# Head pairs: GpSimd forms the low part of every weight tile in two operations of 512 columns in place of one of 1024

## The chip, the cores and the metric

The kernel runs on one core of one Trainium2 chip. The metric is the device time of one execution in microseconds (us). Before the change it is 1581.94 us, the median of three runs (1579.63 to 1582.36).

## The reference

Two blocks of a small model run one after the other on x of 512 tokens by 1024 features, all in float32. Only the first bears on the change:

```python
mod = silu(c) @ w_ada + b_ada                      # shift, scale, gate
h = rms_norm(x, norm_g) * (1.0 + scale) + shift
proj = h @ w_in
(hq, hf, hi, hz, rq, rk, rv, rz, ga, gb) = split(proj)
oA = hgrn2_chunkwise(silu(hq), hf, hi, lower_bounds)        # 8 heads, gated linear recurrence
uA = head_rms_norm(oA, hg_norm_g) * silu(hz)
oB = retention_chunkwise(rotary(rq), rotary(rk), rv)        # 8 heads, retention
uB = head_rms_norm(oB, ret_norm_g) * silu(rz)
m = sigmoid(ga) * uA + sigmoid(gb) * uB
x = x + gate * (m @ w_out)
```

The second block is a conformer convolution, a swiglu FFN, banded attention with sinks and another FFN; the change does not touch it.

## The kernel before

**Split products.** Every float32 weight is used as a sum of two rounded parts. A weight tile (a "chunk", 128 partitions by 1024 columns) is loaded by the sync queue into `w_raw[:, j]`, one of four slots j. ScalarE writes its rounded high part to `w_hi[:, j]` (L791). GpSimd writes the low part, `w_lo = w_raw - w_hi` (`w_low`, L665). TensorE then makes three products for each 128-column block of the chunk: high by high, high by low, low by high (`dense`, L2151 to L2153, features by tokens; `dense_tokens`, L2209 to L2211, which takes two chunks at once and waits for both).

**The stream.** Chunk c sits in slot c mod 4. The semaphore `lo_ready[j]`, which GpSimd raises when a low part is written, does two things: it lets TensorE start on the chunk, and it lets the sync queue load the next chunk into the slot. ScalarE writes a high part when the load has landed (`raw_in[j]`) and TensorE has let go of the slot (`tile_done[j]`). Each engine's order is written out by hand.

**Head pairs.** The first block runs over four pairs of heads, p = 0 to 3, as a loop on each engine. A pair has 20 chunks. Chunks 8 and 9 are taken by VectorE alone, so GpSimd forms the low parts of the others in the order of `LOW_ORDER`: 3, 4, 5, 6, 7, 12, 10, 11, 13 to 19, and then the first three of what comes next (20, 21, 22). That is 18 tiles in a pair and 72 in the loop. Between them stand four 512-column operations (`head_low`, L675) for the head norms: behind chunk 16, behind chunk 17 and two behind chunk 20.

**The place in the middle of a pair.** TensorE's order there is chunk 6, 7, 12, then `hgrn_levels(0)` (L2312), then `dense_tokens` of chunks 10 and 11. The level products are cut over four banks. The first bank waits for the first two levels that VectorE's second loop makes, and the second bank for that loop's last level:

```python
if n < 2:
    pe.wait_ge(prep_done, p * 6 + (3 * e + n + 1))
```

VectorE meanwhile runs `decayed(0)`: seven products of `packed` and `q` (L1509), seven of `packed` and `key` (L1514), the last of which raises `prep_done`, then `k_far` (L1517), a copy of two columns (L1519), `q_far` (L1520), and after it the rotary products L1629, L1630 and L1631. Nearly all of these read two tensors in SBUF. L1631 waits for VectorE's own L1630 to finish; none of the others in this run waits for VectorE itself. ScalarE writes the high part of chunk 10, copies, and then that of chunk 11.

**After the pairs.** GpSimd makes `lead_hi` and `lead_lo` (L684 and L686) behind chunk 22 of the last pair, for the first block of `w_out` on TensorE (L2162).

Of the kernel before, what the change touches and what calls it, by code (L numbers as in the profile page):

```python
# [16 lines left out]
F32 = mybir.dt.float32  # L17
# [3 lines left out]
ALU = mybir.AluOpType  # L21
# [3 lines left out]
T = 512  # L25
# [3 lines left out]
SLOTS = 4  # L29
# [93 lines left out]
PAIR_CHUNKS = 20  # L123
# [5 lines left out]
def phase_starts():  # L129

    sizes = [("pairs", PAIRS * PAIR_CHUNKS), ("w_out", KC), ("pw1", 2 * KC), ("pw2", KC)]
    for layer in range(2):
        if layer == 1:
            sizes += [("kv", 4), ("q", KC), ("w_o", KC)]
        sizes += [(f"up{layer}", 2 * FF_PAIRS), (f"down{layer}", KC)]
    at, starts = 0, {}
    for name, n in sizes:
        assert n % SLOTS == 0
        starts[name] = at
        at += n // SLOTS  # L140
    return starts, at

START, QUADS = phase_starts()
# [47 lines left out]
def program(nc, weights, ada_in, xT, x_turned, vec_in, sinks_in, rel_in, ret_tab, lvl_in, eye_in, tri_in, hot_in, ident_in, taps_in,  # L192
            rel_scratch, glu_scratch, outT):
    ctx = ExitStack()
    with ctx:
        def sb(name, shape, dt=F32, where=ctx):
            return where.enter_context(nc.sbuf_tensor(name, shape, dt))

        def sem(name):
            return ctx.enter_context(nc.semaphore(name))  # L200
# [4 lines left out]
        w_raw = sb("w_raw", [P, SLOTS, D])  # L205
        w_hi = sb("w_hi", [P, SLOTS, D], F32R)
        w_lo = sb("w_lo", [P, SLOTS, D], F32R)
# [129 lines left out]
        hi_ready = [sem(f"hi_ready{j}") for j in range(SLOTS)]  # L337
        lo_ready = [sem(f"lo_ready{j}") for j in range(SLOTS)]
# [318 lines left out]
        def _(pool):  # L657
            TT = nc.gpsimd.tensor_tensor
# [3 lines left out]
            def w_low(I, j):  # L662

                pool.wait_ge(hi_ready[j], I + 1)
                TT(w_lo[:, j, :], w_raw[:, j, :], w_hi[:, j, :].bitcast(F32), ALU.subtract).then_inc(lo_ready[j], 1)  # L665
# [5 lines left out]
            with pool.Fori(0, PAIRS) as p:  # L671
                def head_low(e, r):

                    pool.wait_ge(osq_high, p * 4 + (2 * e + r + 1))
                    TT(osq_lo[:, r, :], hbuf[:, 2 + r, :], osq_hi[:, r, :].bitcast(F32), ALU.subtract).then_inc(osq_low, 1)  # L675

                for c in LOW_ORDER:
                    w_low(p * (PAIR_CHUNKS // SLOTS) + (START["pairs"] + c // SLOTS), c % SLOTS)
                    for e, r in HEAD_LOW_AFTER.get(c, ()):
                        head_low(e, r)  # L680

# [686 lines left out]
        def _(dve):  # L1368
# [401 lines left out]
            def taps(plan):  # L1770

                for c, k, b, last in plan:
# [7 lines left out]
                    else:  # L1780
# [3 lines left out]
                        else:  # L1784
                            STT(conv[:, c, :], src, w, bank, ALU.mult, ALU.add).then_inc(conv_done, 1)

            bank_of = {c: b for run in TAP_PLAN for c, _, b, _ in run}

            def halves_in(c):
# [342 lines left out]
        def _(pe):  # L2132
# [491 lines left out]
            def ffn(layer_n, norm, x_mix, hidden):  # L2624
# [14 lines left out]
                for part in range(MIXED_PARTS):  # L2639
                    lead_down, last_down = (FF_ORDER.index(("down", part, m)) for m in (0, KC // 2 - 1))  # L2640
                    quads(at, lead_down // 2)
                    for n in range(lead_down // 2 * 2, last_down // 2 * 2 + 2):
                        if n == lead_down:
                            pe.wait_ge(hid_low, mixed_at(layer_n, part + 1, 0))
                        kind, _, _ = FF_ORDER[n]
                        seven_products(f0 + n, up + n // 2, n % 2, own_x if kind == "down" else x,
                                       mixes=mixes_before(layer_n, part) if n == lead_down else None)
                    at = last_down // 2 + 1
# [292 lines left out]
```

## Time and profile before

| what | value |
|---|---|
| median of three runs | 1581.94 us (1579.63 to 1582.36) |
| the profiled execution's own time | 1578.51 us |
| its span, first to last instruction | 1576.7 us |
| TensorE busy | 1544.0 us, 98% |
| GpSimd busy | 884.3 us, 56% |
| VectorE busy | 1134.5 us, 72% |
| mean granted TensorE clock | 0.995 of full speed |
| the four head pairs | about 59 to 541 us |

A row of a timeline gives the start in us from the span's start, the duration in us, the engine, the line of the program, the operation, what it writes and reads, the shapes, and in brackets the idle time of the engine before it with what ended that time. "x7" are seven instructions of one line merged into one row. An instruction's duration runs from its start to its end and holds any time in which it was held up inside the engine.

### The profile page before, as it was taken

To read this page: it belongs to the slowest core of one execution; us is meant where nothing else is said; L and a number is where in the kernel's file an instruction comes from. 1 tells how busy PE (TensorE), PEld (TensorE's weight loads), DVE (VectorE), ACT (ScalarE), POOL (GpSimd) and SP (SyncE) were. 2 spreads that over 40 slices of the span, in tenths; PEclk is the share of its full clock that TensorE was granted. 3 is DMA by queue.
4 is the path that set the end of the run, shared out by engine and by line. 5 is a ranking of instruction groups with operands and counts; after the bars stand their busy time and mean duration, and the time that the engine had idled before them with its cause. 6 is when DMAs were issued, how large, how long until landed. Compare 5 with 4: busy or idle time off the path is not lost.

```text
span 1576.7 us, 28481 instructions
## 1 busy us (share of the span) xinstructions
PE 1544.0 (98%) x10803; PEld 1372.8 (87%) x10803; DVE 1134.5 (72%) x1782; ACT 881.7 (56%) x1480; POOL 884.3 (56%) x523
## 2 busy tenths in 40 slices
PE   6999999999999999999999999999999999999997
PEld 4888888888888878568999999988788899999996
DVE  7887587597687869977766766754666766776755
ACT  4555455355355545477664665554667666566553
POOL 1444344445435448827777777654115678677653
PEclk8999999999999999999999999999999999999999
DMA  9422322322323455712333333353112333333332
GB/s 375 144 94 81 121 81 94 120 79 94 116 76 99 136 98 166 188 41 94 107 107 108 107 104 101 104 177 103 54 42 68 98 103 107 106 97 105 108 119 68
DMA packets 53659, 173.12 MB, mean 110 GB/s; under 512 B 5403, under 2 KB 11580, under 8 KB 53052
## 3 DMA queue, kind: packets, MB, share of 16 engines
q1 hardware_dynamic: 47296, 159.90, 32.0%
q10 hardware_dynamic: 6268, 11.95, 3.2%
q8 instruction: 59, 0.97, 0.3%
q14 instruction: 36, 0.29, 0.1%
HBM read 165.48 MB, written 6.36 MB: 109 GB/s over the span
## 4 chain that ended last, share of the span: by engine, by line
PE 79%; DVE 3%; issue 2%; ACT 2%; POOL 2%; DVEq 0%; ACTq 0%; POOLq 0%
PE gps L2151 9%; PE gps L2153 9%; PE gps L2152 9%; PE gps L2588 8%; PE gps L2590 8%; PE gps L2589 8%; PE aps L2588 4%; PE aps L2589 4%; PE aps L2590 4%; PE gps L2511 2%; PE gps L2209 2%; PE gps L2210 1%; PE gps L2211 1%; POOL w_lo L665 1%; PE aps L2678 1%
## 5 line engine op out<-in xcount | busy, mean ns | idle before, releaser
L665 POOL TENSOR_TENSOR w_lo<-w_raw,w_hi 128x1024 fp32r<-128x1024 f32 x140 | 361.1, 2584 | 472.5 <-ACT w_hi L791 472.4
L2151 PE MATMUL gps<-xa_hi,w_hi 128*128 128x512 f32 x639 | 256.8, 402 | 2.5 <-DVE xa_lo L1453 2.5
L2153 PE MATMUL gps<-xa_hi,w_lo 128*128 128x512 f32 x639 | 250.2, 392 | 0.0
L2152 PE MATMUL gps<-xa_lo,w_hi 128*128 128x512 f32 x639 | 250.2, 392 | 0.0
L791 ACT CAST w_hi<-w_raw 128x1024 fp32r<-128x1024 f32 x140 | 146.3, 1045 | 98.6 <-DMA w_raw<-weights_dram 41.7
L2151 PEld LDWEIGHTS gps<-xa_hi,w_hi 128*128 128x128 f32 x639 | 120.5, 189 | 30.5 <-DVE xa_lo L1453 4.1
L2153 PEld LDWEIGHTS gps<-xa_hi,w_lo 128*128 128x128 f32 x639 | 120.6, 189 | 26.2
L2152 PEld LDWEIGHTS gps<-xa_lo,w_hi 128*128 128x128 f32 x639 | 120.8, 189 | 22.6
L1855 DVE TENSOR_TENSOR sums<-aps,sums 128x512 fp32r<-128x512 f32 x58 | 40.1, 692 | 138.4 <-ACT sums L1111 138.4
L746 POOL TENSOR_TENSOR w_lo<-diff,w_hi 128x512 fp32r<-128x512 f32 x60 | 77.7, 1295 | 110.0 <-ACT w_hi L1117 110.0
L740 POOL TENSOR_TENSOR w_lo<-w_raw,w_hi 128x512 fp32r<-128x512 f32 x60 | 92.7, 1545 | 41.6 <-ACT w_hi L1094 41.5
L2151 PE MATMUL gps<-xb_hi,w_hi 128*128 128x512 f32 x250 | 98.4, 394 | 0.0
L2153 PE MATMUL gps<-xb_hi,w_lo 128*128 128x512 f32 x250 | 97.4, 390 | 0.0
L2152 PE MATMUL gps<-xb_lo,w_hi 128*128 128x512 f32 x250 | 97.3, 389 | 0.0
L1845 DVE TENSOR_TENSOR sums<-aps,sums 128x1024 fp32r<-128x1024 f32 x58 | 70.8, 1221 | 17.1 <-ACT sums L1106 16.8
L744 POOL TENSOR_TENSOR w_lo<-w_raw,w_hi 128x512 fp32r<-128x512 f32 x60 | 78.5, 1309 | 0.0
L743 POOL TENSOR_TENSOR diff<-w_raw 128x512 f32<-128x512 f32 x60 | 78.5, 1308 | 0.0
L748 POOL TENSOR_TENSOR w_lo<-w_raw,w_hi 128x512 fp32r<-128x512 f32 x60 | 78.1, 1301 | 0.0
L2588 PE MATMUL gps<-x_blocks,w_hi 128*128 128x256 f32 x264 | 75.5, 286 | 0.0
L2590 PE MATMUL gps<-x_blocks,w_lo 128*128 128x256 f32 x264 | 74.7, 283 | 0.0
L2589 PE MATMUL gps<-x_blocks,w_hi 128*128 128x256 f32 x264 | 74.7, 283 | 0.0
L2209 PE MATMUL gps<-w_hi,xa_hi 128*128 128x256 f32 x256 | 72.8, 284 | 1.8 <-POOL w_lo L665 1.7
(495 smaller groups left out, 5120.9 us busy)
## 6 DMA issues: line engine op xcount, KB each, us to landing
w_raw<-weights_dram SPq DMA_DIRECT2D x268, 512.0 KB, 3.6
ada_w<-ada_in_dram SPq DMA_DIRECT2D x8, 1024.0 KB, 18.6
gates<-ret_tab_dram ACTq DMA_DIRECT2D x4, 1024.0 KB, 6.9
spread<-glu_scratch_dram SPq DMA_DIRECT2D x12, 270.0 KB, 5.0
rel_scratch_dram<-rel_rows ACTq DMA_DIRECT2D x1, 3072.0 KB, 34.5
x<-x_turned_dram SPq DMA_DIRECT2D x2, 1024.0 KB, 7.4
res<-xT_dram ACTq DMA_DIRECT2D x1, 2048.0 KB, 10.3
bias<-rel_scratch_dram ACTq DMA_DIRECT2D x1, 2048.0 KB, 9.1
```

What stands on the lines that cost most here:

```text
L665: TT(w_lo[:, j, :], w_raw[:, j, :], w_hi[:, j, :].bitcast(F32), ALU.subtract).then_inc(lo_ready[j], 1)
L740: TT(lo["w11"], raw["w11"], hi["w11"].bitcast(F32), ALU.subtract).then_inc(first_low, 1)
L743: TT(diff[:], raw["w11"], raw["diff"], ALU.subtract).then_inc(diff_made, 1)
L744: TT(lo["w12"], raw["w12"], hi["w12"].bitcast(F32), ALU.subtract).then_inc(lo_ready[2 * s], 1)
L791: nc.scalar.copy(w_hi[:, j, :], w_raw[:, j, :]).then_inc(hi_ready[j], 1)
L2151: mm(gps[:, j, :], w_hi[:, j, w], x[0][:, k, :], start=k == 0, stop=False)
L2152: mm(gps[:, j, :], w_hi[:, j, w], x[1][:, k, :], start=False, stop=False)
L2153: last = mm(gps[:, j, :], w_lo[:, j, w], x[0][:, k, :], start=False, stop=k == blocks - 1)
L2209: mm(out, x[0][:, k, tok], wh, start=k == 0, stop=False)
L2588: mm(out, highs[s][name][:, w], x[name](k, 0), start=start and k == 0, stop=not start, **more)
L2589: mm(out, highs[s][name][:, w], x[name](k, 1), start=False, stop=not start, **more)
L2590: last = mm(out, lows[s][name][:, w], x[name](k, 0), start=False, stop=not start or k == HALF - 1, **more)
```

## The change

In the loop over the head pairs each low part is written by two operations on the two halves of the columns (T is 512). The wait ahead of the first and the semaphore behind the last stay. The tiles outside the loop, and the four `head_low` operations, are as they were.

```diff
+                def w_low_by_halves(I, j):
+
+                    pool.wait_ge(hi_ready[j], I + 1)
+                    TT(w_lo[:, j, 0:T], w_raw[:, j, 0:T], w_hi[:, j, 0:T].bitcast(F32), ALU.subtract)
+                    TT(w_lo[:, j, T:], w_raw[:, j, T:], w_hi[:, j, T:].bitcast(F32), ALU.subtract).then_inc(lo_ready[j], 1)
+
                 for c in LOW_ORDER:
-                    w_low(p * (PAIR_CHUNKS // SLOTS) + (START["pairs"] + c // SLOTS), c % SLOTS)
+                    w_low_by_halves(p * (PAIR_CHUNKS // SLOTS) + (START["pairs"] + c // SLOTS), c % SLOTS)
```

## Rows read from the trace of the kernel before

**Rows 1.** The page: busy time by engine, and the low parts' group.

```profile
PE 1544.0 (98%) x10803; PEld 1372.8 (87%) x10803; DVE 1134.5 (72%) x1782; ACT 881.7 (56%) x1480; POOL 884.3 (56%) x523
...
L665 POOL TENSOR_TENSOR w_lo<-w_raw,w_hi 128x1024 fp32r<-128x1024 f32 x140 | 361.1, 2584 | 472.5 <-ACT w_hi L791 472.4
```

**Rows 2.** Busy time by engine in the stretch of pair 1.

```profile
179.00:300.00 121.00, 119.21 (x788) 102.48 (x788) 90.81 (x135) 60.02 (x76) 56.44 (x23) 1.00 0.31 97
```

**Rows 3.** Waits of TensorE in the pairs: in total, times, longest (us).

```profile
PE gps L2209 <- POOL w_lo L665: 1.7, 1, 1.7
PE gps L2162 <- POOL osq_lo L686: 0.9, 1, 0.9
```

**Rows 4.** Timeline of GpSimd: low parts with little beside them, pair 0's end.

```profile
142.51 2.54 POOL L675 TENSOR_TENSOR osq_lo<-hbuf,osq_hi 128x512 fp32r<-128x512 f32 x2 [2.83 <-ACT osq_hi L883]
145.01 2.41 POOL L665 TENSOR_TENSOR w_lo<-w_raw,w_hi 128x1024 fp32r<-128x1024 f32 x1
```

**Rows 5.** Timeline of GpSimd: chunk 11 of pair 0, chunks 10 and 11 of pair 2.

```profile
80.87 3.88 POOL L665 TENSOR_TENSOR w_lo<-w_raw,w_hi 128x1024 fp32r<-128x1024 f32 x1 [1.60 <-ACT w_hi L791]
...
316.92 2.51 POOL L665 TENSOR_TENSOR w_lo<-w_raw,w_hi 128x1024 fp32r<-128x1024 f32 x1 [2.85 <-ACT w_hi L791]
321.03 3.91 POOL L665 TENSOR_TENSOR w_lo<-w_raw,w_hi 128x1024 fp32r<-128x1024 f32 x1 [1.59 <-ACT w_hi L791]
```

**Rows 6.** Timeline of VectorE in the same place of pair 2.

```profile
315.08 4.72 DVE L1509 TENSOR_TENSOR packed<-packed,q 128x256 f32<-128x256 f32 x7 [0.99 <-ACT hbuf L875]
319.72 2.50 DVE L1514 TENSOR_TENSOR packed<-packed,key 128x256 f32<-128x256 f32 x7
...
322.61 2.35 DVE L1519 COPY tile_decay<-hbuf 128x2 f32<-128x2 f32 x1
```

**Rows 7.** Timeline of GpSimd: chunks 10 and 11 of pair 1.

```profile
196.13 5.83 POOL L665 TENSOR_TENSOR w_lo<-w_raw,w_hi 128x1024 fp32r<-128x1024 f32 x1 [2.85 <-ACT w_hi L791]
...
201.91 3.95 POOL L665 TENSOR_TENSOR w_lo<-w_raw,w_hi 128x1024 fp32r<-128x1024 f32 x1
```

**Rows 8.** Timeline of VectorE in the same place of pair 1.

```profile
194.28 2.51 DVE L1509 TENSOR_TENSOR packed<-packed,q 128x256 f32<-128x256 f32 x7 [0.99 <-ACT hbuf L875]
...
199.60 2.38 DVE L1519 COPY tile_decay<-hbuf 128x2 f32<-128x2 f32 x1
201.90 0.55 DVE L1520 TENSOR_TENSOR q_far<-q,hbuf 128x384 f32<-128x384 f32 x1
...
202.97 0.68 DVE L1630 TENSOR_TENSOR rqk<-rqk,gates 128x512 f32<-128x512 f32 x1
203.68 2.72 DVE L1631 TENSOR_TENSOR rqk<-rqk,unit 128x512 f32<-128x512 f32 x1
```

**Rows 9.** Timeline of TensorE around the tokens of chunks 10 and 11, pairs 0 to 2.

```profile
82.15 3.29 PE L2312 MATMUL aps<-packed 128*128 128x128 f32 x28
85.20 0.36 PE L2209 MATMUL gps<-w_hi,xa_hi 128*128 128x256 f32 x1
...
206.11 0.36 PE L2209 MATMUL gps<-w_hi,xa_hi 128*128 128x256 f32 x1 [1.67 <-POOL w_lo L665]
...
323.40 1.85 PE L2312 MATMUL aps<-packed 128*64 128x64 f32 x56
325.19 0.38 PE L2209 MATMUL gps<-w_hi,xa_hi 128*128 128x256 f32 x1
```

**Rows 10.** Timeline of ScalarE: the high part of chunk 11 in pair 2.

```profile
319.90 1.05 ACT L791 CAST w_hi<-w_raw 128x1024 fp32r<-128x1024 f32 x1
```

**Rows 11.** Timeline of GpSimd in pair 0: an operation that follows another without a pause.

```profile
114.86 1.46 POOL L675 TENSOR_TENSOR osq_lo<-hbuf,osq_hi 128x512 fp32r<-128x512 f32 x1
```

**Rows 12.** Timeline of VectorE in pair 0 beside it, and its two-column copy undisturbed.

```profile
112.58 2.61 DVE L1509 TENSOR_TENSOR packed<-packed,q 128x256 f32<-128x256 f32 x1
...
115.11 1.58 DVE L1509 TENSOR_TENSOR packed<-packed,q 128x256 f32<-128x256 f32 x1
...
125.03 0.15 DVE L1519 COPY tile_decay<-hbuf 128x2 f32<-128x2 f32 x1
```

**Rows 13.** Timeline of GpSimd behind the last pair: `lead_lo`.

```profile
511.06 1.81 POOL L686 TENSOR_TENSOR osq_lo<-mixed,osq_hi 128x512 fp32r<-128x512 f32 x1
```

## The prediction

> **What bounds the kernel now.** I read the busy times of the page first [rows 1]: TensorE works 98% of the span, so time is lost or won only where TensorE waits. GpSimd is busy for 56%, and its low parts (140 tiles, 72 of them in the pairs, the rest outside) idle 472 us in front of themselves, nearly all of it waiting for ScalarE's high part. Read alone, this says that GpSimd has room and that a slightly dearer low part costs nothing. In the stretch of pair 1 TensorE is busy 119.2 of 121 us and GpSimd 56.4 [rows 2]. The waits of TensorE in all four pairs are two of any size: 1.7 us for a low part, once, and 0.9 us behind the last pair for `lead_lo` [rows 3].
>
> The one wait leads to the place that matters: the tokens of chunks 10 and 11. In pair 1 the low part of chunk 11 ends at 201.91 + 3.95 = 205.86 and TensorE goes on at 206.11, 0.25 to 0.26 later, after 1.67 us idle [rows 7, 9]. In pair 2 it ends at 321.03 + 3.91 = 324.94 and TensorE goes on at 325.19 [rows 5, 9]: the same 0.25, though no idle time shows. So this low part arrives just in time there, with no slack; pair 3 repeats pair 2. In pair 0 it ends at 84.75 and TensorE goes on at 85.20, a slack of about 0.2 [rows 5, 9]. Every delay here is paid in full, four times. All other low parts in the pairs end 3 us or more before their use; the two 512-column operations behind chunks 16 and 17 have over 1 us.
>
> **Why chunk 11 is late.** ScalarE has its high part at 319.90 + 1.05 = 320.95 in pair 2 [rows 10]. An unhindered low part takes 2.41 [rows 4], yet this one takes 3.91. VectorE tells why: its copy of two columns takes 2.35 us there, against 0.15 in another place [rows 6, 12], and both end together at 324.96. The two engines shut each other out while both read SBUF. GpSimd got its turn only when VectorE reached the copy at 322.61; the copy then waited out GpSimd. VectorE's instructions before it follow each other without a pause (14 of 0.41 us at a spacing of 0.34, plus `k_far`); I call this a train. A GpSimd operation that meets a train has two fates. In pair 2 chunk 10 comes at 316.92 and is let in at once (2.51), and the seven L1509 take 4.72 in place of 2.51 [rows 5, 6, 8]. In pair 1 it comes at the same offset from the train's start (1.85) and is kept out for the whole train, until the copy at 199.60: 5.83 [rows 7, 8]. Chunk 11, right behind it, loses again: `q_far`, L1629 and L1630 pass, and it gets in at 203.65, where L1631 waits for its predecessor and leaves a gap (L1631 then takes 2.72). These two fates set the price of a second operation.
>
> **The change, part by part.** *Work added.* Two operations of 512 columns back to back take 2.54 with nothing beside them, one of 1024 takes 2.41 [rows 4]: 0.13 more, 72 times, 9 us of GpSimd's time. Away from chunks 10 and 11 it is hidden behind TensorE's products, by the slacks above.
>
> *The second half must win its turn again.* Two outcomes stand in the trace. (a) One VectorE instruction slips in: at 114.86 a GpSimd operation follows another, the L1509 that was blocked finishes at 112.58 + 2.61 = 115.19, the next (115.11) is blocked for 1.58, and GpSimd's operation takes 1.46 in place of 1.27 [rows 4, 11, 12]. The tile then costs 1.3 + 1.46 = 2.75, about 0.3 more. (b) The train passes: chunk 11 of pair 1, above, lost 203.65 - 201.95 = 1.7 us [rows 7, 8].
>
> *Chunk 10 in pairs 0, 2 and 3.* The blocked instruction is a 256-column product, as in (a), so I take (a): it ends 0.3 later, which nobody waits for, since ScalarE's high part holds back chunk 11 until 320.95. VectorE's total block stays near 2.3, as it does one instruction in between.
>
> *Chunk 11 in pairs 0, 2 and 3.* If it still comes in at the copy, the first half ends 1.25 after 322.61, at 323.86. Behind the copy is the very situation of pair 1, so (b): `q_far`, L1629, L1630, 1.7 us; the second half runs from 325.56 to 326.8, 1.85 later than now. With (a) it is one `q_far` (0.5) and 0.1: 0.55 later. If chunk 11 is instead let in inside the train (the train stands 0.1 us elsewhere than before, which can turn the outcome), it is early, but the last L1514 is blocked about 2.4 us, from 322.2 to 324.6. The second bank of levels needs it after 16 of 56 products, at 323.40 + 0.47 = 323.87 [rows 9]: 0.7 us late. In pair 0 TensorE needs it at 82.15 + 8 of 28 products (0.9) = 83.05 and would get it at 84.4: 1.4 us. So the cost is 0.55 at the least and 1.85 at the most, by either way; I take 1.1, between the ends, three times: 3.3 us.
>
> *Pair 1.* If chunk 10 is kept out again until 199.60, its halves and those of chunk 11 need four turns instead of two. With (a) each time it ends about 0.3 later than now. With (b) each time: first half to 200.85, second from 202.55 (behind L1630) to 203.8, chunk 11 from the next gap at 205.5 to 206.8, and from the gap behind that (207.4) to 208.7: 2.8 later than 205.86. I take 1.3.
>
> *The rest of the pair.* Chunk 7's low part blocks VectorE's scans and chunk 12's a one-column addition; halves hold the port as long in all, and I put this at 0, at most 0.1. The loads behind `lo_ready` are 0.1 to 0.3 us later, hidden since ScalarE's high parts wait for TensorE to free the slot. Behind the last pair `lead_lo` takes 1.81 because it waits for a VectorE product [rows 13]; a start 0.25 later ends at the same time. Bounds: 0 and 0.3; I take 0.
>
> *Sum.* 3.3 + 1.3 = 4.6 us. The profiled execution's own time is 1578.51 (span 1576.7, and 1.8 around it); it becomes 1583.1. The median of the runs lies 3.4 above that execution, so the forecast is 1581.9 + 4.6 = 1586.5.
>
> **A rule beside it.** The Trainium skill, "SBUF — State Buffer", section "SBUF: two separate sides", says of the ports that VectorE and GpSimd share: whoever starts first has them for the whole instruction, and the other is fully blocked. By that rule, the lock free at each instruction's end, a half would wait for one VectorE instruction and never for a train. The copy's 2.35 us agree with the rule, chunk 10 of pair 1 does not: ten VectorE instructions passed it.
>
> **The rivals.** *One instruction only.* If each half waits for a single VectorE instruction, outcome (a) holds everywhere: 0.4 us in pair 0, 0.55 in pairs 2 and 3, 0.3 in pair 1, together 1.8: 1583.7, not to be told from no change. For it: the row at 114.86, which its repetitions in the later pairs confirm. Against it: both low parts of pair 1. This is also what the rule above would give.
>
> *The other side: not slower.* The change shifts when GpSimd asks, and whether chunk 10 is let in at once in pair 1 hangs on a few hundredths of a us. If it is, and the halves of chunk 11 fit in without delay, pair 1's 1.67 us go and nothing comes: 1580.3. It decides once chunk 11 ends no later than 0.25 us before TensorE's need in all pairs. All idle time of TensorE that GpSimd causes in the pairs is 1.7 + 0.9 = 2.6 us, so more than 0.2% (3.2 us) is out of reach.
>
> *The train wins always.* The second half of chunk 10 loses to the train too, in pairs 0, 2 and 3: it gets in at the copy (about 321.5) and ends at 322.75; then chunk 11's first half waits for the gap behind L1630 (324.5) and its second for the next one (327.6), ending at 328.9. That is 3.9 us a pair, with pair 1's 2.8 together 14.5: 1596.4. For it: the 5.83 us row. Against it: 114.86.
>
> **How the numbers follow.** 0.2% (3.2 us) is about what a measurement of this kernel can tell from no change. The forecast, a loss of 1.5 to 8 us, has 0.55, of which a fifth lies under 3.2. The rivals near no change (-1.7 to +1.5, with 1583.7 at their edge) have 0.25 together. The train has 0.15. I leave 0.05 for faster by more than 3.2, which no row supports. Slower is 0.44 + 0.15 = 0.59, same 0.11 + 0.25 = 0.36. The forecast's own range is 1583.4 to 1590; with the cases on both sides the range is 1580.5 to 1594.
>
> **What the profile would show.** Right: L665 in two forms, 144 instructions of about 1.3 us in the pairs; new waits of `dense_tokens` for `w_lo` in pairs 0, 2 and 3, of 0.5 to 1.9 us, or waits of L2312 for L1514 in their place; second halves of 2.5 to 3 us where they lose. Wrong: second halves of 1.3 to 1.5 us throughout and no new wait (the first rival); the L1509 group of 4.72 back at 2.5 to 3.6 with a second half of over 3 us (the last). What would make the prediction wrong is above all the arbitration, which four places of one execution show, and whose outcome turned with nothing visible between pairs 1 and 2.

## The result and the profile after

The changed kernel takes 1582.69 us in the median of 18 runs, the kernel before, run beside it on the same chip, 1579.24 in the median of 18 (1576.49 to 1582.36). The ratio is 1.0019, with a 95% interval of 1.001 to 1.0028: 3.0 us slower, between 1.6 and 4.4. That is a loss, but a small one, just inside the 0.2% that I had called no difference. Two of the 18 executions, of 1687.83 us (mean granted clock 0.849) and 3066.96 us, are left out of the ratio (the median of the other 16 is 1582.08), and nothing found below explains them.

The profiled execution after took 1586.11 (span 1584.3), the one before 1578.51 (span 1576.7). These two differ by 7.6 us, more than the medians do. Much of what follows is about why. First the page of the kernel after, the lines that answer to [rows 1], and its table of costliest groups:

```profile
PE 1544.6 (97%) x10803; PEld 1374.8 (87%) x10803; DVE 1111.6 (70%) x1782; ACT 881.7 (56%) x1480; POOL 907.7 (57%) x595
...
L665 POOL TENSOR_TENSOR w_lo<-w_raw,w_hi 128x1024 fp32r<-128x1024 f32 x68 | 166.6, 2456 | 222.3 <-ACT w_hi L797 222.2
L680 POOL TENSOR_TENSOR w_lo<-w_raw,w_hi 128x512 fp32r<-128x512 f32 x72 | 111.5, 1549 | 239.3 <-ACT w_hi L797 238.9
L681 POOL TENSOR_TENSOR w_lo<-w_raw,w_hi 128x512 fp32r<-128x512 f32 x72 | 109.8, 1525 | 0.0
```

The change was made: 144 halves, of 1.54 us on average where two back to back with nothing beside them take 1.27 [rows 4]. GpSimd is busy 23.4 us longer and VectorE 22.9 us shorter: a blocked VectorE instruction counts as busy, and short halves block it for less. All lines behind the change stand 6 lower (L1509 is now L1515, L1514 is L1520, L1519 is L1525, L2209 is L2215, L2312 is L2318).

Waits of TensorE in the pairs, after, as in [rows 3] (total, times, longest, in us), for the stretch from 54 us on, which begins a little earlier than mine of before did:

```profile
PE gps L2215 <- POOL w_lo L681: 6.9, 3, 2.8
PE gps L2168 <- POOL osq_lo L692: 1.0, 1, 1.0
PE aps L2318 <- DVE packed L1520: 0.4, 1, 0.4
```

Three waits for the second half of a low part where before had one. The timeline of TensorE places them: pair 0's first tokens, then chunks 10/11 of pair 1 (which waits for VectorE instead) and of pair 2. Pair 3, at 450.46 with 2.77, repeats pair 2.

```profile
55.38 0.35 PE L2215 MATMUL gps<-w_hi,xa_hi 128*128 128x256 f32 x1 [1.30 <-POOL w_lo L681]
...
204.57 1.39 PE L2318 MATMUL aps<-packed 128*64 128x64 f32 x40 [0.36 <-DVE packed L1520]
205.89 0.39 PE L2215 MATMUL gps<-w_hi,xa_hi 128*128 128x256 f32 x1
...
327.48 0.36 PE L2215 MATMUL gps<-w_hi,xa_hi 128*128 128x256 f32 x1 [2.78 <-POOL w_lo L681]
```

**Chunks 10 and 11, pair 1: let in.** GpSimd's timeline, then VectorE's, to be held against [rows 7] and [rows 8]:

```profile
197.02 1.42 POOL L680 TENSOR_TENSOR w_lo<-w_raw,w_hi 128x512 fp32r<-128x512 f32 x1 [2.71 <-ACT w_hi L797]
198.40 1.55 POOL L681 TENSOR_TENSOR w_lo<-w_raw,w_hi 128x512 fp32r<-128x512 f32 x1
201.12 1.30 POOL L680 TENSOR_TENSOR w_lo<-w_raw,w_hi 128x512 fp32r<-128x512 f32 x1 [1.17 <-ACT w_hi L797]
202.38 1.47 POOL L681 TENSOR_TENSOR w_lo<-w_raw,w_hi 128x512 fp32r<-128x512 f32 x1
```

```profile
198.72 5.80 DVE L1520 TENSOR_TENSOR packed<-packed,key 128x256 f32<-128x256 f32 x7
204.44 0.55 DVE L1523 TENSOR_TENSOR k_far<-key,hbuf 128x384 f32<-128x384 f32 x1
204.91 0.16 DVE L1525 COPY tile_decay<-hbuf 128x2 f32<-128x2 f32 x1
```

Chunk 10 gets in at once, and chunk 11 gets in too, inside VectorE's train. It is early, done at 203.85. The two halves stretch the seven L1520 to 5.80 us; TensorE's second bank of levels waits 0.36 for the last of them. The 1.67 of before are gone here.

**Pair 2: kept out.** GpSimd's timeline against [rows 5], VectorE's against [rows 6]:

```profile
316.31 4.74 POOL L680 TENSOR_TENSOR w_lo<-w_raw,w_hi 128x512 fp32r<-128x512 f32 x1 [2.71 <-ACT w_hi L797]
321.01 2.87 POOL L681 TENSOR_TENSOR w_lo<-w_raw,w_hi 128x512 fp32r<-128x512 f32 x1
323.84 1.71 POOL L680 TENSOR_TENSOR w_lo<-w_raw,w_hi 128x512 fp32r<-128x512 f32 x1
325.51 1.71 POOL L681 TENSOR_TENSOR w_lo<-w_raw,w_hi 128x512 fp32r<-128x512 f32 x1
```

```profile
316.90 2.51 DVE L1520 TENSOR_TENSOR packed<-packed,key 128x256 f32<-128x256 f32 x7
...
319.80 1.28 DVE L1525 COPY tile_decay<-hbuf 128x2 f32<-128x2 f32 x1
320.99 0.55 DVE L1526 TENSOR_TENSOR q_far<-q,hbuf 128x384 f32<-128x384 f32 x1
```

The first half of chunk 10 waits for the whole train, until the copy at 319.80. Then the second half loses again: three VectorE instructions pass and it takes 2.87. This is outcome (b) of the prediction, but on chunk 10. The halves of chunk 11 let one 512-column instruction by each (1.71), and end at 327.22; TensorE goes on 0.26 later.

The starts of TensorE's tokens serve as marks for a whole run. T4 is the first matmul of the tokens of chunks 4/5 of a pair, T10 that of chunks 10/11. The distances (differences of starts in TensorE's timeline, us) split the whole 7.6:

```
                 T4 of 0 |pair 0|10->4 |pair 1|10->4 |pair 2|10->4 |pair 3|10->lead|rest
before             54.22 |30.98 |89.44 |31.48 |89.34 |29.74 |89.36 |29.75 |68.63   |1063.8
after              55.38 |30.99 |89.21 |30.31 |89.00 |32.59 |90.41 |32.58 |69.80   |1064.1
after - before     +1.16 | 0.0  |-0.23 |-1.17 |-0.34 |+2.85 |+1.05 |+2.83 |+1.17   |+0.2
```

The kept-out pairs 2 and 3 cost 2.85 and 2.83 themselves, and the stretches behind them 1.05 and 1.17 more, where the same stretches behind pairs 0 and 1 are shorter than before. The experiments take these columns one by one.

### The profile page after: what moved, and what is told of

Same layout as the page of the kernel before. It is cut to its first block, busy times and chain, and to the rows that moved or that the text cites. A ratio compares the mean times of both kernels' runs of the same rounds, so it can differ in the third digit from the quotient of the medians.

```text
span 1584.3 us, 28553 instructions
## 1 busy us (share of the span) xinstructions
PE 1544.6 (97%) x10803; PEld 1374.8 (87%) x10803; DVE 1111.6 (70%) x1782; ACT 881.7 (56%) x1480; POOL 907.7 (57%) x595
## 4 chain that ended last, share of the span: by engine, by line
PE 65%; DVE 3%; ACT 2%; issue 1%; POOL 1%; DMA 0%; ACTq 0%; DVEq 0%
PE gps L2594 8%; PE gps L2596 8%; PE gps L2595 8%; PE gps L2157 6%; PE gps L2159 6%; PE gps L2158 6%; PE aps L2594 4%; PE aps L2595 4%; PE aps L2596 4%; PE gps L2517 2%; PE aps L2684 1%; PE aps L2694 1%; PE gps L2706 1%; PE gps L2215 1%; PE gps L2217 1%
## 5 line engine op out<-in xcount | busy, mean ns | idle before, releaser
L665 POOL TENSOR_TENSOR w_lo<-w_raw,w_hi 128x1024 fp32r<-128x1024 f32 x68 | 166.6, 2456 | 222.3 <-ACT w_hi L797 222.2
L680 POOL TENSOR_TENSOR w_lo<-w_raw,w_hi 128x512 fp32r<-128x512 f32 x72 | 111.5, 1549 | 239.3 <-ACT w_hi L797 238.9
L746 POOL TENSOR_TENSOR w_lo<-w_raw,w_hi 128x512 fp32r<-128x512 f32 x60 | 92.7, 1545 | 41.5 <-ACT w_hi L1100 41.5
L681 POOL TENSOR_TENSOR w_lo<-w_raw,w_hi 128x512 fp32r<-128x512 f32 x72 | 109.8, 1525 | 0.0
L2215 PE MATMUL gps<-w_hi,xa_hi 128*128 128x256 f32 x256 | 74.2, 290 | 6.9 <-POOL w_lo L681 6.9
L750 POOL TENSOR_TENSOR w_lo<-w_raw,w_hi 128x512 fp32r<-128x512 f32 x60 | 78.5, 1309 | 0.0
L754 POOL TENSOR_TENSOR w_lo<-w_raw,w_hi 128x512 fp32r<-128x512 f32 x60 | 78.1, 1302 | 0.0
L2594 PE MATMUL gps<-x_blocks,w_hi 128*128 128x256 f32 x264 | 75.5, 286 | 0.0
```

The costliest lines, as they stand in the source:

```text
L680: TT(w_lo[:, j, 0:T], w_raw[:, j, 0:T], w_hi[:, j, 0:T].bitcast(F32), ALU.subtract)
L681: TT(w_lo[:, j, T:], w_raw[:, j, T:], w_hi[:, j, T:].bitcast(F32), ALU.subtract).then_inc(lo_ready[j], 1)
L746: TT(lo["w11"], raw["w11"], hi["w11"].bitcast(F32), ALU.subtract).then_inc(first_low, 1)
L2215: mm(out, x[0][:, k, tok], wh, start=k == 0, stop=False)
L2594: mm(out, highs[s][name][:, w], x[name](k, 0), start=start and k == 0, stop=not start, **more)
```

## Experiments

Each group of kernels was run beside the kernel before, whose medians were 1577.81 (e1 to e4, 25 runs), 1579.85 (e5 to e8, 35) and 1579.11 (e9 to e11, 17); each ratio is against the runs beside it, with its 95% interval in brackets.

**1 and 2. Halves at chunks 10 and 11 alone, and everywhere but there.** The edits in GpSimd's loop over `LOW_ORDER`:

```
-                    w_low_by_halves(p * ..., c % SLOTS)
+                    low = w_low_by_halves if c in (10, 11) else w_low      # e1
+                    low = w_low_by_halves if c not in (10, 11) else w_low  # e2
+                    low(p * ..., c % SLOTS)
```

> Only chunks 10 and 11 are written in two halves (8 of the 72 tiles); the others in one operation as before. My theory after the two traces: the loss of the change has two parts, one at chunks 10 and 11 (a pair whose chunk 10 is kept out by VectorE's train costs 2.8 us of TensorE's time where it cost 1.7, a pair whose chunk 10 is let in costs 0 to 0.4 where it cost 0) and one at chunks 4 and 5 of pair 0 (1.2 us). This kernel has the first part alone: about 2 us above the kernel before in the median, a spread of single executions of about 8 us and more (it was 6 before), no wait of 1.3 us at the first tokens of pair 0. Rival, the cost is in the number of operations (each adds 0.13 us or more somewhere): 8 of 72 tiles give 0.3 us.

> All tiles but chunks 10 and 11 in halves (64 of 72). My theory: the 1.2 us at chunks 4 and 5 of pair 0 remains, the kept-out pairs cost 1.7 us each as before: 1.2 us above the kernel before, the spread of single executions about 6 us as before, a wait of 1.2 to 1.3 us at the first tokens of pair 0. Rival, the cost is in the number of operations: 2.7 us, nearly all of the change's loss.

Measured: halves at 10 and 11 alone 1584.05 us (6 runs), ratio 1.0042 [1.0029, 1.0055]; everywhere else 1578.5 (12 runs), 1.0002 [0.9994, 1.0011]. So the loss sits in eight of the 72 tiles. That there are more operations costs nothing as a whole: the 64 other tiles, split, leave the time where it was. In e1 pair 0 was kept out (its waits, from the timeline of TensorE):

```profile
89.86 0.35 PE L2216 MATMUL gps<-w_hi,xa_hi 128*128 128x256 f32 x1 [2.43 <-POOL w_lo L681]
```

That pair 0 takes 33.66 from T4 to T10, 2.68 more than before. In e10 below, where the other tiles are in halves too, a kept-out pair 0 takes only 31.51, with a wait of 0.28: VectorE's train starts 18.49 us behind T4 there and 20.67 in e1, so most of the same delay falls before TensorE's need.

The other three pairs of e1 were let in: 30.32 to 30.33 from T4 to T10, 0.58 above the 29.74 of a whole-tile pair that is let in. I had expected e1 about 2 us above the kernel before; the ratio says 6.6 (4.6 to 8.7). It lacks the gain described next, and its kept-out pair 0 is dear; measured terms and a chance give 5.1 for it (see the sum near the end).

Two things in e2 I had not expected. Pair 0's first tokens wait 1.30 there as in the kernel after, and in e1 they don't (0.13). And the stretches from T10 to the next T4 take 88.94 to 89.18, 0.3 to 0.4 less than before. The one hides the other in e2's ratio.

**3 and 4. A pause in the train.** VectorE waits for its own seventh product before the eighth, in the kernel before (e3) and after (e4):

```
-PAIR_STEPS = 29
+PAIR_STEPS = 31
...
-                        TT(q_part, q_part, right(qe, level), ALU.mult)
+                        last = TT(q_part, q_part, right(qe, level), ALU.mult)
+                    own.done(last)
```

> The kernel before, with one wait more on VectorE: behind the seventh product L1509 VectorE waits for its end before L1514 starts, in both uses of the function. My theory, that an operation of GpSimd which misses its turn is kept out until VectorE pauses: the train of 15 instructions now has a pause behind the seventh, so chunk 10 gets in at the latest 0.5 us after it asks, no low part of chunk 10 takes more than 3.2 us (5.8 was seen), TensorE's wait of 1.7 us is gone from every pair, and the times lie near the lowest of the kernel before: 2 to 3 us below its median, with a spread of single executions of 2 us or less in place of 6. Rival, the spread and the wait come from something else (loads, ScalarE): the median and the spread stay, or the pause itself costs TensorE 0.1 to 0.5 us a pair.

> The changed kernel with the same pause on VectorE. My theory: no pair is kept out, so what is left of the change is the 1.2 us at pair 0's first tokens and 0 to 0.4 us a pair where the last L1514 comes late for the second bank of levels: 1 to 2.5 us above the kernel before with the pause, about 0.5 us below the kernel before, spread 2 us or less. Rival, the kept-out pairs are no cause: 3 us above the kernel before, with the spread of the changed kernel (11 us).

Measured: e3 1582.81 (7 runs), 1.0029 [1.0018, 1.004], slower and not faster; e4 1579.61 (11 runs), 1.0012 [1.0003, 1.0021]. I had expected both below the kernel before, e3 by 2 to 3 us and e4 by 0.5; both lie above it, e4 by 1.9 (0.5 to 3.3). In both, all four pairs were let in at once. In e4 that took the spread of the runs from 10.8 us (1578.36 to 1589.11, the two left out aside) to 2.3 (1578.73 to 1581.04): the spread of the kernel after is mostly the fate of chunk 10. In e3 another thing came up. Timelines of GpSimd and VectorE, pair 2:

```profile
319.28 2.52 POOL L665 TENSOR_TENSOR w_lo<-w_raw,w_hi 128x1024 fp32r<-128x1024 f32 x1 [2.85 <-ACT w_hi L791]
323.39 2.50 POOL L665 TENSOR_TENSOR w_lo<-w_raw,w_hi 128x1024 fp32r<-128x1024 f32 x1 [1.59 <-ACT w_hi L791]
```

```profile
317.44 4.73 DVE L1509 TENSOR_TENSOR packed<-packed,q 128x256 f32<-128x256 f32 x7 [0.99 <-ACT hbuf L875]
322.20 4.70 DVE L1515 TENSOR_TENSOR packed<-packed,key 128x256 f32<-128x256 f32 x7
```

Now the whole chunk 11 also gets in inside the train, and the product that it blocks is the one that TensorE needs: waits of 1.18 in pair 0 and 0.51 in the others. The prediction had priced this case at 1.4 and 0.7. An early low part is no gain where the one who pays for it is later.

**5, 6 and 7. Both turns given by hand.** On top of the pause, GpSimd waits for VectorE's last product of the first head before chunk 11, so it starts at the copy as in [rows 5, 6]. e5 has whole tiles, e7 halves for all but 3, 4 and 5, e6 halves for all but 3, 4, 5, 10 and 11:

```
+                    if c == 11:
+                        pool.wait_ge(prep_done, p * 6 + 2)
+                    low = w_low_by_halves if c not in (3, 4, 5, 10, 11) else w_low  # e6
+                    low = w_low_by_halves if c not in (3, 4, 5) else w_low          # e7
```

> The kernel before (no halves) with two waits more: VectorE pauses behind the seventh L1509, and GpSimd starts the low part of chunk 11 only when VectorE's last L1514 of the first head is done. My theory: the fates of both low parts are fixed now. Chunk 10 is let in at once in all four pairs (as with the pause alone), chunk 11 gets in at the copy of two columns behind the train, so the last L1514 is not late (the 0.7 us a pair and 1.4 in pair 0 of the pause alone are gone) and chunk 11 ends as in the let-in pairs of the kernel before. From the first tokens of a pair to its second tokens: 31.0 us in pair 0 and 29.7 to 29.8 in the others, none at 31.5. Time: 1.67 us below the profiled execution of the kernel before at the same start-up, about 1577 us, or 1579 where TensorE's first sums run at the lower granted clock (1.9 us, a matter of chance in every kernel). Rival, the order is not what costs: as the kernel with the pause alone, 1582.8 us.

> The same two waits, and the halves for all chunks but 3, 4, 5, 10 and 11. My theory: the halves cost where two of them must win their turn against VectorE on the path to TensorE (chunks 4 and 5 of pair 0, chunks 10 and 11), and gain about 0.35 us a pair elsewhere (from the second tokens of a pair to the first of the next: 89.0 in place of 89.35 us), so this version keeps the gain alone: 1 to 1.5 us below the kernel before with the two waits, 2 to 3 us below the kernel before, spread of single executions about 2 us. Rival, the 0.35 us come with something else of the two halved kernels: no gain over the two waits alone.

> As the last one, but chunks 10 and 11 in halves too; the only difference is how many turns these two need. This puts my prediction's step to the test: the first half of chunk 11 gets in at the copy, behind which q_far, L1629 and L1630 follow without a pause. If a train passes a waiting GpSimd (outcome b of the prediction), the second half comes 1.7 us later and TensorE waits 1.7 to 1.9 us in each pair, 6 to 8 us in all, more if TensorE's clock falls behind the waits. If one instruction passes (outcome a), 0.5 us a pair, 2 us in all. The second half behind the copy in the kept-out pairs of the changed kernel took 2.87 us, so I expect the first.

Measured (12 runs each): e5 1579.36, 0.9993 [0.9983, 1.0003]; e6 1576.64, 0.9985 [0.9975, 0.9995]; e7 1582.85, 1.0019 [1.0009, 1.0029]. The step from e6 to e7 is the disputed one by itself: halves for chunks 10 and 11, with both turns fixed. Timelines of GpSimd and VectorE in e7, pair 2:

```profile
323.38 1.54 POOL L680 TENSOR_TENSOR w_lo<-w_raw,w_hi 128x512 fp32r<-128x512 f32 x1 [2.45 <-DVE packed L1524]
324.88 2.85 POOL L681 TENSOR_TENSOR w_lo<-w_raw,w_hi 128x512 fp32r<-128x512 f32 x1
```

```profile
323.69 1.26 DVE L1529 COPY tile_decay<-hbuf 128x2 f32<-128x2 f32 x1
324.87 0.54 DVE L1530 TENSOR_TENSOR q_far<-q,hbuf 128x384 f32<-128x384 f32 x1
325.33 0.68 DVE L1639 TENSOR_TENSOR unit<-unit,gates 128x512 f32<-128x512 f32 x1
325.94 0.68 DVE L1640 TENSOR_TENSOR rqk<-rqk,gates 128x512 f32<-128x512 f32 x1
326.65 1.64 DVE L1641 TENSOR_TENSOR rqk<-rqk,unit 128x512 f32<-128x512 f32 x1
```

The second half, right behind the first, loses to three instructions and takes 2.85; TensorE waits 1.63, the same in pairs 1 and 3. From T4 to T10 it is 31.43 against 29.83 in e6: 1.6 us a pair. The medians differ by 6.2 us, of which the four pairs give 5.2. Outcome (b) stands, at its price, where chunk 11 comes in at the copy. In pair 0 the wait is 0.14 only, and the stretch 31.37 against 30.99.

e6 beats both kernels, by 0.15% the one before (interval 0.05% to 0.25%). Its only wait for GpSimd in the pairs is the 0.9 for `lead_lo`. Against e5 it shows what halves are worth where they do no harm. The place is VectorE's `gates` product at L1665 (L1672 in e6). Timelines of GpSimd and VectorE in e5, pair 2:

```profile
367.63 2.37 POOL L665 TENSOR_TENSOR w_lo<-w_raw,w_hi 128x1024 fp32r<-128x1024 f32 x1 [3.82 <-ACT w_hi L793]
```

```profile
368.50 2.05 DVE L1665 TENSOR_TENSOR gates<-gates,unit 128x512 f32<-128x512 f32 x1
...
376.87 0.74 DVE L1563 COPY_PREDICATED at_near<-eye_mask,aps 128x512 f32<-128x512 int32 x1 [0.26 <-DVE at_near L1550]
```

and in e6:

```profile
364.95 1.29 POOL L680 TENSOR_TENSOR w_lo<-w_raw,w_hi 128x512 fp32r<-128x512 f32 x1 [3.74 <-ACT w_hi L800]
366.19 1.73 POOL L681 TENSOR_TENSOR w_lo<-w_raw,w_hi 128x512 fp32r<-128x512 f32 x1
```

```profile
365.91 0.88 DVE L1672 TENSOR_TENSOR gates<-gates,unit 128x512 f32<-128x512 f32 x1
...
373.15 0.74 DVE L1570 COPY_PREDICATED at_near<-eye_mask,aps 128x512 f32<-128x512 int32 x1 [0.26 <-PE aps L2322]
```

A whole tile blocks the product for 2.05 us, a half for 0.88. Between the product's start and the end of the `eye` copy lie 9.11 us in e5 and 7.98 in e6, and in e6 the copy no longer waits for VectorE itself but for TensorE. The attention behind it starts earlier: from T10 to the next T4 88.94 in e6, 89.31 to 89.32 in e5 (pairs 1 and 2), and behind the last pair 68.29 against 68.62. TensorE shows the same place: behind T10 of pair 2 its matmuls keep step in the two kernels, until `aps<-at_r,val` some 52 us later, which starts 0.3 us earlier in e6, and from the next one on 0.36. The medians of e5 and e6 differ by 2.7 us, twice the 1.3 that the four stretches give: the runs of each kernel fall in two groups about 2 us apart (a matter of the start, see below), and 7 of 12 runs of e5 but 5 of 12 of e6 are in the upper one.

**8. The kernel after with chunks 3, 4 and 5 whole.** The edit is `c not in (3, 4, 5)` alone, with no pause and no wait.

> The changed kernel with chunks 3, 4 and 5 in one operation again (60 of 72 tiles in halves), nothing else. My theory: the wait of 1.3 us at the first tokens of pair 0 falls to 0.1, the rest stays as in the changed kernel: 1.2 us below it in the median, a wide spread as there (10 us), since each pair whose chunk 10 is kept out still costs 2.8 us, and 1.4 more for a lower granted clock behind the wait. Rival: the wait at the first tokens of pair 0 has another origin and stays.

Measured: 1580.05 (12 runs, 1577.08 to 1586.1), 1.0006 [0.9994, 1.0019]. The first tokens of pair 0 wait 0.17 in place of 1.30. All four pairs of its profiled execution were let in.

**9. Chunk 11 later still.** e6, with chunk 11 waiting for VectorE's next signal, `pool.wait_ge(rot_ready, p * 2 + 1)`, to see whether a longer wait of TensorE costs its length alone.

> The ordered version without halves for chunks 3, 4, 5, 10 and 11 (the one that took 1576.6 us), but GpSimd waits for VectorE's first L1631 before it starts chunk 11, about 5 us later. This makes one known wait of TensorE in each pair and asks what it costs beyond its own length: in the changed kernel two waits of 2.8 us were each followed by a stretch in which the granted clock read 0.77 and TensorE lost 1.4 us more, while waits of 1.6, 1.7 and 2.4 us in other kernels were not. Theory: the low part of chunk 11 ends near 14.7 us from the start of the train in place of 10.0, a wait of 4.7 us in each of pairs 1 to 3 and 3.5 in pair 0, and the clock falls behind each, 1.4 us or more every time: 17.5 us of waits and some 6 us of clock, 1600 us. Rival: the low clock there was chance, 1594 us.

Measured: 1593.41 (4 runs), 1.0082 [1.0063, 1.0102]. The waits came out shorter than I had worked out, 1.54 in pair 0 and 3.04, 2.93 and 3.05 in the others. Behind each of the three long ones, and not behind the 1.54, the stretch up to the next T4 is longer as well: 90.45 and 90.43, and 69.72 behind the last, against 88.94 and 68.29 in e6. The time itself lies at the number of my rival (1594, no lower clock), but only because the waits are 10.6 us in all in place of 17.5; the stretches behind them, 4.4 us longer in all, decide for the clock.

**10 and 11. The kernels after and before once more,** for a second sample of fates.

> The changed kernel once more, for four more pairs. Theory: every pair shows one of the two courses seen: let in (from the pair's first tokens to its second 30.3 us, last L1514 at 9.3 us from the train's start) or kept out (32.6 us, waits of 2.8 us, 1.4 us of lower clock behind it); the time is 1578.4 + 3.7 for each kept-out pair + 0 or 1.9 for the start. Rival: a third course, or kept-out pairs without the lower clock.

> The kernel before once more, for four more pairs. Theory: let in 29.74 us or kept out 31.5 us from first to second tokens (31.0 in pair 0), no lower clock behind a wait of 1.7; the time is 1576.8 + 1.7 for each kept-out pair among pairs 1 to 3 + 0 or 1.9 for the start. Rival: a pair with a wait above 2 us, so that the changed kernel's 2.8 us are no work of the halves.

Measured: after 1583.43 (6 runs), 1.0014 [0.9997, 1.003], its profiled execution 1589.3; before 1579.71 (8 runs), 1.0003 [0.9992, 1.0014]. In e10 pairs 0, 1 and 2 were kept out and pair 3 was let in; in e11 only pair 2 was kept out, with a wait of 1.68 (in [rows 7] it was pair 1). Pair 0 of e10 is the third course that my rival asked for: kept out, but with a wait of 0.28 and no lower clock behind it. The same program meets another fate in the same pair of another execution.

**A lower clock behind the longest waits.** Busy time by engine, granted clock, DMA share and GB/s of short stretches behind the 2.78 us wait of pair 2 in the kernel after:

```profile
327.50:328.50 1.00, 1.00 (x8) 1.00 (x9) 0.97 (x3) 0.00 (x0) 0.00 (x0) 0.96 0.24 37
328.50:329.50 1.00, 1.00 (x7) 1.00 (x6) 0.81 (x2) 0.97 (x1) 0.00 (x0) 0.50 0.87 238
329.50:330.50 1.00, 1.00 (x7) 1.00 (x7) 0.71 (x2) 0.07 (x1) 0.85 (x1) 0.50 0.99 393
330.50:331.50 1.00, 1.00 (x6) 1.00 (x6) 0.64 (x2) 0.00 (x0) 1.00 (x2) 0.50 0.95 348
331.50:332.50 1.00, 1.00 (x9) 1.00 (x8) 0.80 (x2) 0.00 (x0) 0.67 (x1) 0.83 0.08 33
332.50:333.50 1.00, 1.00 (x11) 1.00 (x10) 1.00 (x1) 0.00 (x0) 0.00 (x0) 1.00 0.43 49
```

TensorE is busy throughout, but during about 3.4 us (twice what the shares lack of 1.00) it runs at the lower of its two levels, 1.2 GHz, and gets through fewer matmuls. The stretch from T10 to the next T4 is 90.41 against 88.98 in e4, pair 2, where the same halves were let in: 1.43 us. The same follows in the other pairs with waits of 2.77 or more:

| wait of TensorE (us) | where | 10->4, or 10->lead | same stretch, let in |
|---|---|---|---|
| 1.54 | e9 pair 0 | 89.19 | 89.18 (e6) |
| 1.6 | e7 pairs 1 to 3 | 88.94, 88.95, 68.31 | 88.94, 88.94, 68.29 (e6) |
| 2.43 | e1 pair 0 | 89.46 | 89.47 (e5) |
| 2.78, 2.77 | after, pairs 2, 3 | 90.41, 69.80 | 88.98, 68.34 (e4) |
| 2.79, 2.78 | e10 pairs 1, 2 | 90.43, 90.42 | 88.99, 88.98 (e4) |
| 3.04, 2.93, 3.05 | e9 pairs 1 to 3 | 90.45, 90.43, 69.72 | 88.94, 88.94, 68.29 (e6) |

## Why the prediction was off

It said slower, by 4.6 us, with 1586.5 as the time and 1580.5 to 1594 as the range. The sign was right, the time lies in the range, and the loss of 3.0 us is smaller. Against the 1579.24 of the 18 runs beside it, 1586.5 would be 7.3 us more, where 3.0 were measured. What failed, in short: the base of the sum, a median of three runs, which lay 2.7 us too high and makes most of the 3.8 us by which the time was missed; the fate of chunk 10, which the sum tied to its pair; the lower clock behind a kept-out pair of halves (1.43 us), which had no term; and two terms put at nothing, the first tokens of pair 0 (+1.2 us) and the rest of the pairs (-1.3 us). The mechanism, a second turn that the second half must win, was right (e7 shows it, at 1.6 us). One by one:

**The base.** "The median of the runs lies 3.4 above that execution, so the forecast is 1581.9 + 4.6 = 1586.5." That median was of three runs, drawn high. Over 18 it is 1579.24, only 0.7 above the profiled execution. Runs of the kernel before lie between 1576.3 and 1583.2, with two causes that the profiles show: each pair of 1 to 3 in which chunk 10 is kept out costs 1.74 (31.48 against 29.74), and TensorE's first sums at 13 us take twice as long in some executions, such as e1, whose T4 of pair 0 comes 2.0 us later than in the kernel before. I had 1.67 us of the first cause before my eyes and took it for a property of pair 1. The second cause, in TensorE's timelines of the kernel before and of e1:

```profile
12.89 1.13 PE L2248 MATMUL aps<-lnv,ones_r 128*128 128x512 f32 x2 [1.52 <-DVE lnv L1428]
13.86 1.02 PE L2250 MATMUL aps<-sq,ones_r 128*128 128x512 f32 x2
```

```profile
13.10 2.08 PE L2255 MATMUL aps<-lnv,ones_r 128*128 128x512 f32 x2 [1.58 <-DVE lnv L1435]
14.96 1.91 PE L2257 MATMUL aps<-sq,ones_r 128*128 128x512 f32 x2
```

```profile
14.04 1.91 PE L2257 MATMUL aps<-sq,ones_r 128*128 128x512 f32 x2
```

```profile
15.00:16.00 1.00, 1.00 (x6) 0.12 (x8) 0.51 (x3) 0.00 (x0) 0.53 (x1) 0.50 1.00 397
```

So the slow sums are the lower clock level in e8, and by their durations in the others too. What varies is how much of the first 30 us runs at that level: in e6 the sums are slow (2.08 and 1.92), but the matmuls from 26 to 28 us are fast (0.40 in place of 0.63), and T4 of pair 0 stands at 54.23, as in the kernel before. What sets it from one execution to the next is open. The change has no part in it, since both durations are found in kernels with and without it.

**Pair 1, "I take 1.3".** There was no place-bound pair 1. In my trace it happened to be the pair that was kept out, in e11 it was pair 2, in e2 pairs 0, 2 and 3. Over all profiled executions without the pause, 5 of 12 pairs of whole tiles at chunks 10 and 11, and 6 of 16 of halves, were kept out. The terms should have been made for each fate, and weighed with a chance in every pair. The size was near: in a kept-out pair TensorE's stretch grows by 1.1, from 31.48 to 32.59, before the clock is counted.

**Chunk 11 in pairs 0, 2 and 3, "0.55 at the least and 1.85 at the most, by either way; I take 1.1".** Mis-sized when chunk 10 is let in: chunk 11's halves then get in inside the train, the case that I had named and priced at 1.4 in pair 0 and 0.7 in the others. It costs 0 and 0.57 (30.3 against 29.74). With whole tiles, in e3, it costs 1.44 and 0.7. In pair 0 the difference is that with all tiles in halves the train starts 18.5 us behind T4 in place of 20.7, partly because T4 itself is late. The 1.6 of (b) at the copy is real, as e7 shows, but the kernel after does not come to the copy. Missing when chunk 10 is kept out: outcome (b) then strikes chunk 10's second half (2.87), and the halves of chunk 11 follow. Of chunk 10 itself, "it ends 0.3 later, which nobody waits for" held in the pairs let in (0.4 later).

**The clock.** Not in the sum at all: a kept-out pair of halves brings TensorE's wait from 1.67 to 2.78, and behind it another 1.43 are lost. With the 1.1 that makes 2.5 us a kept-out pair, more than I took for any pair.

**"All other low parts in the pairs end 3 us or more before their use."** Wrong for one tile (a few others end 2.8 us before, which costs nothing). In pair 0 chunk 5's low part ended in the kernel before at

```profile
51.38 2.58 POOL L665 TENSOR_TENSOR w_lo<-w_raw,w_hi 128x1024 fp32r<-128x1024 f32 x1
...
54.22 0.36 PE L2209 MATMUL gps<-w_hi,xa_hi 128*128 128x256 f32 x1
```

(timelines of GpSimd and of TensorE), that is 53.96, and TensorE went on at 54.22, the same 0.26 that I had read as "no slack" elsewhere. No list of waits named it, as its wait is 0.13 us. In the kernel after the four halves there (1.39, 1.47, 1.74, 1.71) end at 55.12, and the wait is 1.30. e2 and e8 confirm it, with and without those halves: a loss of 1.2 us, once.

**The rest of the pair, "Bounds: 0 and 0.3; I take 0."** It was a gain. The stretches without chunks 10 and 11 got 0.23 to 0.4 shorter each (halves against whole tiles in every kernel of this study), 1.3 us in all. I had the right instruction kind in view (VectorE blocked by chunks 7 and 12), but looked only at who waits for GpSimd; the gain goes to those who wait for VectorE.

The sum again, by measured terms and a chance of 0.4 for kept out: first tokens +1.2; pair 0 +0.2 (0.4 × 0.5); pairs 1 to 3, each 0.6 × 0.57 + 0.4 × 2.5 = 1.34, +4.0; the rest -1.3. That is 4.1 us, in the measured 1.6 to 4.4 near its upper end. (For e1 the first and last terms are nothing and pair 0 is +1.1, 0.4 × 2.7: 5.1 in all.) The chance is a count of 28 pairs in seven executions (11 kept out), so this sum is an account and no test. The forecast's 4.6 is near it by offsetting errors, not by its terms: that is luck.

**The rivals.** "The train wins always" did not come: it wins 4 times in 10, and the halves do not make that more frequent as far as 28 pairs tell. "One instruction only", which would also follow from the rule of the Trainium skill, "SBUF — State Buffer", section "SBUF: two separate sides", fits the second halves that let one instruction by (1.55 in pair 1 of the kernel after) and fails again elsewhere: the half at 316.31 is passed by the rest of a train. "Not slower" named the event that happened in pair 1 of the kernel after (-1.17), and missed that the same draw can go the other way elsewhere.

**What stays open.** What decides between let in and kept out. GpSimd's request comes 1.84 to 1.86 us behind the start of the train, 0.15 to 0.18 behind the start of the VectorE instruction of the moment, in both fates. Without the pause 17 of 28 pairs were let in at once and 11 were kept out for the whole train; with it 21 of 24 were let in at once, 3 at the pause itself, and none was kept out for the whole train. That the pause ends a wait is shown by those three. Whether it also makes a wait rarer (3 of 24 against 11 of 28), though it lies behind the moment at which GpSimd asks, the counts suggest and do not show.

## What to carry to other kernels

Splitting an operation on GpSimd that shares its port with VectorE buys shorter blocks for VectorE and pays with one more turn to be won; so split where VectorE's result is the one awaited, keep whole where the low part is, and give the turn by a semaphore at the one or two places where a train decides (e6, 0.15% faster than the kernel before). Look for places that are just in time by the constant distance between a producer's end and its user's start (0.25 us here), not by the list of waits, and look in the first pass of a loop too. When two fates stand in one trace of the same code, count them over several executions before either is put into a sum, and expect the median of three runs to carry that draw.

## What the hardware showed that I had not expected

- Behind each of seven waits of TensorE of 2.77 to 3.05 us the granted clock fell to 1.2 GHz for about 3.4 us, which cost about 1.43 us more; behind waits of 1.5 to 1.6, and one of 2.43, it did not. A stall that grew by 1.1 us cost 2.5.
- The grant of the shared port looks like a draw: the same request at the same offset was let in within 0.2 us, or held back for 3.4 to 3.5 us (5.83 - 2.41, 4.74 - 1.27) while VectorE's instructions passed, in 11 of 28 pairs. With a wait of VectorE for its own product in the middle of the train no request was held back for longer than 0.6 us in 24 pairs, and the wait cost nothing that shows (30.3 from T4 to T10 in e4 and in the kernel after).
- A 512-column half costs 1.27 to 1.30 us alone, 1.46 to 1.57 with a 256-column VectorE instruction let by in front of it, 1.71 with a 512-column one, and 2.85 to 2.89 with three.
